# Feed-forward down products in pairs of slices, with seven block products for half of the columns

## The reference, cut to what matters

```
h = h + 0.5 * (silu(u @ wg) * (u @ wu)) @ wd        # u = rmsnorm(h), D = 1024, F = 2816
```

## Time and profile before

| | us |
|---|---|
| median of 3 runs | 1896.27 (1895.78 to 1896.41) |
| profiled execution, span | 1894.6 |
| its own time beside the span | not given; the median is 1.7 above the span |
| PE busy, DVE busy, ACT busy | 1874.1, 1229.6, 945.6 |

### The profile page before, as it was taken

The page is one execution under the profiler, slowest core; times in us unless marked ns, Lnnn a source line. Parts: engine busy times, 40 slices in busy tenths (PEclk is TensorE's granted clock), DMA queues, the critical chain, the costliest instruction groups (busy, mean ns, idle before and its releaser), DMA issues.

```text
span 1894.6 us, 34284 instructions
## 1 busy us (share of the span) xinstructions
PE 1874.1 (99%) x13508; PEld 1745.4 (92%) x13508; DVE 1229.6 (65%) x1654; ACT 945.6 (50%) x1301; POOL 66.1 (3%) x94
## 2 busy tenths in 40 slices
PE   9999999999999999999999999999999999999998
PEld 8999999999998889999999998999999998889998
DVE  5666765675556647666765699765676665877665
ACT  5444544454446636444544457644454446455443
POOL 0000100000000000000100000100010002010000
PEclk9999999999999999999999999999999999999999
DMA  7555455545453245555555443565545453344552
GB/s 282 199 191 184 164 199 199 189 165 207 185 198 134 68 149 215 191 183 194 200 199 198 146 145 111 201 233 199 189 167 203 185 199 126 130 152 178 192 199 100
DMA packets 61505, 338.60 MB, mean 179 GB/s; under 512 B 6976, under 2 KB 7360, under 8 KB 33024
## 3 DMA queue, kind: packets, MB, share of 16 engines
q1 hardware_dynamic: 59472, 330.00, 47.3%
q0 software_dynamic: 1968, 7.70, 1.2%
HBM read 336.62 MB, written 1.05 MB: 178 GB/s over the span
## 4 chain that ended last, share of the span: by engine, by line
PE 93%; DVE 3%; ACT 2%; issue 1%; POOL 1%; DMA 1%; SPq 0%; DVEq 0%; ACTq 0%; POOLq 0%
PE X L1698 55%; PE Y L1698 36%; DMA rawA<-in_wa 1%; ACT hiA L590 1%; PE X L1739 1%; ACT arena L804 0%; DVE arena L1481 0%; DVE xs L1193 0%; DVE h L1200 0%; DVE xl L1145 0%; PE Y L2213 0%; DVE loA L1105 0%; DVE arena L1418 0%; POOL ms_eps L489 0%; PE X L1722 0%
## 5 line engine op out<-in xcount | busy, mean ns | idle before, releaser
L1698 PE MATMUL X<-xh,hiA 128*128 128x256 f32 x2464 | 679.0, 277 | 1.7 <-DVE loA L1091 0.8
L1698 PE MATMUL X<-xl,hiA 128*128 128x256 f32 x2464 | 677.4, 277 | 0.0
L1698 PE MATMUL X<-xh,loA 128*128 128x256 f32 x2464 | 668.9, 277 | 0.0
L1105 DVE TENSOR_TENSOR loA<-rawA,hiA 128x2048 fp32r<-128x2048 f32 x213 | 487.9, 2290 | 265.2 <-ACT hiA L590 265.0
L1698 PEld LDWEIGHTS X<-xh,hiA 128*128 128x128 f32 x2464 | 462.7, 188 | 3.2 <-DVE loA L1091 1.7
L1698 PEld LDWEIGHTS X<-xl,hiA 128*128 128x128 f32 x2464 | 463.3, 188 | 0.0
L1698 PEld LDWEIGHTS X<-xh,loA 128*128 128x128 f32 x2464 | 457.1, 188 | 0.0
L590 ACT ACTIVATE hiA<-rawA 128x2048 fp32r<-128x2048 f32 (+1 forms) x239 | 424.0, 1776 | 46.1 <-PE Y L1698 29.8
L708 ACT ACTIVATE act_s<-act_s 128x256 f32<-128x256 f32 x154 | 64.4, 418 | 427.2 <-DVE act_s L1257 427.2
L1698 PE MATMUL Y<-hiB,act_hh 128*128 128x512 f32 x704 | 275.5, 391 | 0.9 <-DVE act_hl L1270 0.9
L1698 PE MATMUL Y<-hiB,act_hl 128*128 128x512 f32 (+1 forms) x880 | 275.9, 346 | 0.0
(11 more groups left out here) (263 smaller groups left out, 2217.8 us busy)
## 6 DMA issues: line engine op xcount, KB each, us to landing
rawA<-in_wa SPq DMA_DIRECT2D x221, 1024.0 KB, 5.4
rawB<-in_wb SPq DMA_DIRECT2D x181, 512.0 KB, 3.5
row_gain<-in_rows POOLq DMA_DIRECT2D x8, 512.0 KB, 6.1
arena<-in_gla POOLq DMA_DIRECT2D x1, 1280.0 KB, 5.8
h<-in_x SPq DMA_DIRECT2D x2, 512.0 KB, 4.0
arena<-in_taps POOLq DMA_DIRECT2D x1, 576.0 KB, 5.7
arena<-in_pool POOLq DMA_DIRECT2D x1, 544.0 KB, 6.6
rawA<-in_wa SPq DMA_DIRECT2D x2, 256.0 KB, 5.9
```

What stands on the lines that cost most here:

```text
L1105: nc.vector.tensor_tensor(loA[p][:, :], rawA[p][:, :], hiA[p][:, :].bitcast(f32), ALU.subtract).then_inc(a_lo, 1)
L1698: return say(nc.tensor.matmul(*args, **kw))
```

## The change

Slice 0 and the slices 19, 20, 21 are done as before. The 18 slices between go in PAIRS = 9 pairs (1,2), (3,4) ... (17,18), on PE: gate_up of the next odd slice, gate_up of the next even one, then the down products of a pair.

The right 512 output columns of a pair are done as before, undivided in the last matmul. The left 512 form a product of 2 x 2 blocks (2 token halves, 2 slices; 2 slices, 2 column blocks of 256), done by seven block products instead of eight, in Winograd's form of Strassen's scheme. DVE makes four sums of weights (T1 to T4, the first two in one operation) and four of activations (S1 to S4); ACT and DVE split them in high and low parts too, which lie in xh and xl or oh2 and ol2, whichever the stage doesn't use. Three of the seven products go straight to their places in Y; four are collected in X banks 2 and 3 over all nine pairs (the one in X[:, 2, 0:256] goes into all four places of the result). Once in each feed-forward `fold` forms the sums of the collected blocks that the four places need, splits them, and PE adds them into Y by four matmuls of 512 with the identity.

Gate and up of a slice now share one bank of X, and DVE scales both in one operation after up. act_hh, act_hl, hiB and loB are made for both slices of a pair in one operation. The SP queue loads in the order A, B, B, A. In ffn0 the weighing of the pool weights stands in the last period, before the scaling of slice 20. The copy of ident_r moves on POOL from the stage before the latent attention to the start of the kernel; the wait before the latent keys and before the attention's scores counts one less.

```diff
+        def gate_bank(p):
+            return X[:, p, 0:TOKENS]
+        def up_bank(p):
+            return X[:, p, TOKENS:2 * TOKENS]
+        sums_w = xs[:, 1, :].rearrange("p (a b) -> p a b", b=TOKENS)
+        sums_act = xs[:, 0, 0:512].rearrange("p (a b) -> p a b", b=P)
+        fold_raw = xs[:, 1, :]
+        fold_tmp = xs[:, 0, 512:512 + TOKENS]
...
+        def spare(s):
+            pair = (xh, xl) if s["reuse"] else (oh2, ol2)
+            return [v.rearrange("p a b -> p (a b)") for v in pair]
+        def pair_w(s, i):
+            return [v[:, TOKENS * i:TOKENS * (i + 1)] for v in spare(s)]
+        def pair_act(s, i):
+            return [v[:, 1024 + P * i:1024 + P * (i + 1)] for v in spare(s)]
...
+                    def later_loads(i):
+                        load_A(a + 4 + 2 * i, a % 2)
+                        load_B(b + 1 + 2 * i, (b + 1) % 2)
+                        load_B(b + 2 + 2 * i, b % 2)
+                        load_A(a + 5 + 2 * i, (a + 1) % 2)
+                    with sp.Fori(1, PAIRS) as i:
+                        later_loads(i)
+                    taken[0] = a + NF
+                    later_loads(PAIRS)
+                    load_B(b + NF - 1, (b + 1) % 2)
...
+                    nc.gpsimd.tensor_copy(ident_r[:, :], ident[:, :]).then_inc(ident_r_set, 1)
...
+                def pair_hi(i):
+                    act.wait_ge(prod_done, e + 1 + 2 * i)
+                    act.wait_ge(b_free, b + 1 + 2 * i)
+                    nc.scalar.activation(act_hh[:, :, :], act_h[:, :, :], ACT.Copy).then_inc(prod_hi, 2)
+                    act.wait_ge(pair_sums, SUMS * (pairs + i))
+                    nc.scalar.activation(act_sum_hi, sums_act.rearrange("p a b -> p (a b)"), ACT.Copy
+                                         ).then_inc(sum_act_hi, 1)
+                    for f in (1, 2):
+                        act.wait_ge(b_loaded[(b + f) % 2], loads(b + f - 2 + 2 * i, (b + f) % 2))
+                    nc.scalar.activation(hiB_both[:, :, :], rawB_both[:, :, :], ACT.Copy).then_inc(b_hi, 2)
+                    nc.scalar.activation(w_hi, sums_w.rearrange("p a b -> p (a b)"), ACT.Copy).then_inc(sum_w_hi, 1)
+                def period(i):
+                    pair_hi(i)
+                    silu(2 * i + 1, 1)
+                    split_A(a + 3 + 2 * i, (a + 1) % 2)
+                    silu(2 * i + 2, 0)
+                    split_A(a + 4 + 2 * i, a % 2)
...
+                period(PAIRS)
+                product_hi(NF - 3, 1, NF - 1)
+                nc.scalar.activation(fold_raw[:, TOKENS:2 * TOKENS], X[:, 2, 0:TOKENS], ACT.Copy).then_inc(fold_copied, 1)
+                split_B(b + NF - 3, (b + 1) % 2)
+                product_hi(NF - 2, 0, NF - 1)
+                for half in range(2):
+                    act.wait_ge(fold_sums, 4 * s["ffn"] + 2 + 2 * half)
+                    nc.scalar.activation(w_hi[:, HALF[half]], fold_raw[:, HALF[half]], ACT.Copy).then_inc(fold_hi, 1)
+                split_B(b + NF - 2, b % 2)
+                silu(NF - 1, 1)
+                product_hi(NF - 1, 1, NF)
+                split_B(b + NF - 1, (b + 1) % 2)
+                split_A(a + NF + 1, (a + 1) % 2)
...
+                def scaled(f, p, opened=False):
                     if s["late"]:
...
                         dve.wait_ge(up_psum, e + 1 + f)
...
+                        both = X[:, p, :].rearrange("p (a b) -> p a b", b=TOKENS)
...
+                def weight_sums(i):
+                    if not (isinstance(i, int) and i == 1):
+                        dve.wait_ge(sum_w_lo, pairs - 1 + i)
+                    for f in (1, 2):
+                        dve.wait_ge(b_loaded[(b + f) % 2], loads(b + f - 2 + 2 * i, (b + f) % 2))
+                    flat = rawB_both.rearrange("p a b -> p (a b)")
+                    taken = flat[:, TOKENS:TOKENS + 1536].rearrange("p (a b) -> p a b", b=768)[:, :, 0:TOKENS]
+                    upper = rawB[0][:, 0:TOKENS].rearrange("p (a b) -> p a b", a=1).broadcast_to([P, 2, TOKENS])
+                    nc.vector.tensor_tensor(sums_w[:, 0:2, :], upper, taken, ALU.subtract).then_inc(pair_sums, 1)
+                def act_sums(i):
+                    done = SUMS * (pairs - 1 + i)
+                    def after(n):
+                        dve.wait_ge(pair_sums, done + n)
+                    if not (isinstance(i, int) and i == 1):
+                        dve.wait_ge(sum_act_lo, pairs - 1 + i)
+                    a11, a21 = (act_h[:, one, P * t:P * t + P] for t in range(TT))
+                    a12, a22 = (act_h[:, two, P * t:P * t + P] for t in range(TT))
+                    dve.wait_ge(prod_done, e + 1 + 2 * i)
+                    nc.vector.tensor_tensor(sums_act[:, S1, :], a21, a22, ALU.add).then_inc(pair_sums, 1)
+                    nc.vector.tensor_tensor(sums_act[:, S3, :], a21, a11, ALU.subtract).then_inc(pair_sums, 1)
+                    after(1)
+                    nc.vector.tensor_tensor(sums_w[:, T2, :], rawB[1][:, 0:TOKENS], sums_w[:, T1, :], ALU.subtract
+                                            ).then_inc(pair_sums, 1)
+                    after(2)
+                    nc.vector.tensor_tensor(sums_act[:, S2, :], sums_act[:, S1, :], a11, ALU.subtract).then_inc(pair_sums, 1)
+                    after(4)
+                    nc.vector.tensor_tensor(sums_w[:, T4, :], rawB[1][:, TOKENS:2 * TOKENS], sums_w[:, T2, :], ALU.subtract
+                                            ).then_inc(pair_sums, 1)
+                    after(5)
+                    nc.vector.tensor_tensor(sums_act[:, S4, :], a12, sums_act[:, S2, :], ALU.subtract).then_inc(pair_sums, 1)
...
+                def period(i, last=False):
+                    split_A(a + 2 + 2 * i, a % 2)
+                    dve.wait_ge(prod_hi, e + 1 + 2 * i)
+                    nc.vector.tensor_tensor(act_hl[:, :, :], act_h[:, :, :], act_hh[:, :, :].bitcast(f32),
+                                            ALU.subtract).then_inc(prod_lo, 2)
+                    dve.wait_ge(sum_act_hi, pairs + i)
+                    nc.vector.tensor_tensor(act_sum_lo, sums_act.rearrange("p a b -> p (a b)"), act_sum_hi.bitcast(f32),
+                                            ALU.subtract).then_inc(sum_act_lo, 1)
+                    dve.wait_ge(b_hi, b + 1 + 2 * i)
+                    nc.vector.tensor_tensor(loB_both[:, :, :], rawB_both[:, :, :], hiB_both[:, :, :].bitcast(f32),
+                                            ALU.subtract).then_inc(b_lo, 2)
+                    dve.wait_ge(prod_lo, e + 1 + 2 * i)
+                    scaled(2 * i + 1, 1)
+                    dve.wait_ge(sum_w_hi, pairs + i)
+                    nc.vector.tensor_tensor(w_lo, sums_w.rearrange("p a b -> p (a b)"), w_hi.bitcast(f32),
+                                            ALU.subtract).then_inc(sum_w_lo, 1)
+                    product(2 * i + 1, 1)
+                    split_A(a + 3 + 2 * i, (a + 1) % 2)
+                    if last and a == 0 and plan[1]["kind"] == "pool":
+                        weigh_pooling(plan[1]["a"])
+                    scaled(2 * i + 2, 0)
                     if not last:
+                        weight_sums(i + 1)
+                    product(2 * i + 2, 0)
+                    if not last:
+                        act_sums(i + 1)
...
+                def fold():
+                    done = 4 * s["ffn"]
+                    p5, p6, p7 = X[:, 2, TOKENS:2 * TOKENS], X[:, 3, 0:TOKENS], X[:, 3, TOKENS:2 * TOKENS]
+                    place = [fold_raw[:, TOKENS * q:TOKENS * (q + 1)] for q in range(4)]
+                    dve.wait_ge(b_free, b + NF - 1)
+                    dve.wait_ge(sum_w_lo, pairs + PAIRS)
+                    dve.wait_ge(fold_copied, s["ffn"] + 1)
+                    nc.vector.tensor_tensor(fold_tmp, place[1], p6, ALU.add).then_inc(fold_sums, 1)
+                    dve.wait_ge(fold_sums, done + 1)
+                    nc.vector.tensor_tensor(place[0], fold_tmp, p5, ALU.add).then_inc(fold_sums, 1)
+                    nc.vector.tensor_tensor(place[3], fold_tmp, p7, ALU.add).then_inc(fold_sums, 1)
+                    dve.wait_ge(fold_sums, done + 3)
+                    nc.vector.tensor_tensor(place[2], place[3], p5, ALU.add).then_inc(fold_sums, 1)
+                def fold_low():
+                    for half in range(2):
+                        dve.wait_ge(fold_hi, 2 * s["ffn"] + half + 1)
+                        nc.vector.tensor_tensor(w_lo[:, HALF[half]], fold_raw[:, HALF[half]],
+                                                w_hi[:, HALF[half]].bitcast(f32), ALU.subtract).then_inc(fold_lo, 1)
...
+                product_lo(0, 0)
+                if s["reuse"]:
+                    latent_lo()
+                split_A(a + 2, a % 2)
+                scaled(1, 1)
+                product(1, 1)
+                split_A(a + 3, (a + 1) % 2)
+                scaled(2, 0)
+                weight_sums(1)
+                product(2, 0)
+                act_sums(1)
```

(108 more changed lines are left out.)

125 lines of the change are left out of this document (66 added, 59 removed).

## The result

The changed kernel takes **1919.05 us**, median of 4 runs (1918.37 to 1919.62), against 1896.03 (1895.24 to 1896.41) for the kernel before beside it: ratio 1.0119, 95% interval 1.0105 to 1.0133. It is slower by 23.0 us. The forecast was 1886.3, faster by 10.0, with 1897.0 as the top of its range: wrong in sign, and by 32.8 us in size. The profiled execution's span went from 1894.6 to 1916.6 us.

What follows compares the result with a forecast made beforehand. PE's matmul starts were taken as the bound: -25.1 us (pairs), +7.3 (fold), +2.1 (beginning), +5.3 (tail), +0.9 (ffn0), -0.5 (old tail wait) gave -10.0, hence 1886.3 us; 8 in 10 range 1879 to 1897.

Steps and rivals of the forecast that it cites:

- The step that failed: PE's steady period: starts cost 0.445 ns a column at either width, so two slices' gate and up take 10.92 us.
- The narrow products: Left half of a pair's down products: 21 matmuls of 256 columns at 0.1138 us each, 2.39 us.
- rival 4: In the pairs, 256-wide down matmuls start slower than gate/up's: 9.5 us if all 21 do, 1895.8, no change; 8%.
- Rival 5: On PE, each matmul has a price apart from its columns: at 30 ns each 19 us, 1906; 1%.
- The gain of seven for eight: Pairs' down products on PE: 5.13 us instead of 5.48, 0.35 less, over 72 pairs -25.1 us.
- The cover in the middle: Steady pairs: DVE's 14.3 us and ACT's 8.8 hide within PE's 16.05 us period, least margin 3.5 us.
- Rival 1: Steady pairs: B loads become the loop if two land over 7.1 us after issue; at 7.5 us, 1909; 9%.
- The two ends: Feed-forward's beginning and tail: PE waits 0.3 us (+2.1 in all) and 0.75 us (+5.3), plus 0.9 in ffn0.
- the tail's walk: After the last pair, a chain through DVE and ACT makes PE wait 0.75 us at slice 21, 7 times: +5.3.
- Rivals 2 and 3: Feed-forward ends: either they cost nothing (1878, 9%), or 2.5 us more a feed-forward (1904; half of that 1895; 12%).

Runs made afterwards that it cites:

- experiment 1: The kernel before, with the last down matmul of each slice left undivided as one of 512 columns: 1924.18 us, ratio 1.0145.
- experiment 4: The changed kernel with each pair's narrow products first, then its twelve wide matmuls, the last one divided into two of 256: 1893.45 us, ratio 0.9984.
- 3: The changed kernel with each pair's narrow products first, then its twelve wide matmuls, all undivided: 1919.16 us, ratio 1.0118.
- experiment 2: The changed kernel with the last wide matmul of a pair divided in its old place, ahead of the narrow products: 1920.12 us, ratio 1.0123.
- 7: The kernel before, with both the last and the last but one down matmul of a slice divided: 1898.30 us, one run.
- 6: The kernel before, with the division moved to the last but one of a slice's twelve down matmuls: 1898.25 us, one run.
- 5: The kernel before, with the division moved from the last to the first of a slice's twelve down matmuls: 1929.25 us, one run.

## Why the prediction was wrong, point by point

**The step that failed** is the one on which the period's sum stands: "The cost goes by columns, 0.445 ns each, at either width", and from it "10.92 of gate and up of the two next slices". It read the pitch of the earlier trace rows as a property of a 256-wide matmul. It is a property of that sequence: the same matmuls take 113.4 to 113.9 ns or 117.8, by what stands ahead of them, and in the changed kernel the 96 of two slices take 11.31 us and not 10.92. The change "removed" the division of the last wide matmul; I counted it as the same columns in one start less, at no cost and no gain, and gave it no bounds. Taken away alone in the kernel before, it costs 27.8 us (experiment 1); put back near gate in the changed one it gives 25.7 (experiment 4 against 3). Put back in its old place it gives nothing (experiment 2, 1920.12 us): the change had also put 21 narrow matmuls between it and gate, and either of the two would have been enough for the long rhythm. Bounds for it could have been had from the trace: the same shape at its other pitch, 0.19 us a slice.

**The narrow products** (forecast 2.39 us a pair) take 2.48. That is rival 4, which I had at 8% and 9.5 us: 120 ns were feared, 118 measured, (2.48 - 2.39) x 72 = 6.5 us. Its row, the start at 0.12 us after a change of width, was the right hint; that whole stretches of gate and up could run so stood in no rival. Gate and up alone lose 8 x 0.39 + 0.19 us a feed-forward, 26.5 us in all, more than the gain of 25.1 that the pairs were to bring, and that decides the sign. A row against the rule was in the trace of before all along, 5.65 us for 48 starts, outside the loop on which the sum was made.

**Rival 5**, a price of each matmul apart from its columns, isn't the cause: most of the loss lies in gate and up, which got no start more, and in experiment 1 one start less made the kernel slower. That a start is free is not shown, though. One start more went with 0.01 us more in experiment 2 against the changed kernel (2.77 against 2.76), 0.02 in the kernel before against 1 (2.74 against 2.72), and nothing in 7 against 6 (2.75 both). The largest step is 5 against 1, both long: 1929.25 against 1924.18 us, 5.1 us for 160 starts, some 32 ns each, with one run of 5. The prediction's count was wrong as well: a pair has 33 starts against 26, seven more and not nine, 504 in all, and the fold's 32 make the 536. An estimate from the gap figures of the Trainium skill (TensorE: Matmul & The Clock Gate, Back-to-back issue gap) had the pair's products cost 0.49 us more than before. They cost 5.24 against 5.48, and no run here bears those figures out.

**The gain of seven for eight** was right in sign: with the short rhythm in gate and up and long narrow matmuls the prediction's sum is 1886.3 + 6.5 = 1892.8, and experiment 4 measured 1893.45.

**The cover in the middle** held. The timeline of DVE (start, duration, engine, line, operation):

```profile
101.28 2.29 DVE L1423 TENSOR_TENSOR loB<-rawB,hiB 128x2048 fp32r<-128x2048 f32 x1 [1.03 <-ACT hiB L782]
...
104.40 1.21 DVE L1428 TENSOR_TENSOR ol<-xs,oh 128x1024 fp32r<-128x1024 f32 x1
...
106.77 2.29 DVE L1203 TENSOR_TENSOR loA<-rawA,hiA 128x2048 fp32r<-128x2048 f32 x1 [0.82 <-ACT hiA L651]
...
110.05 0.68 DVE L1386 TENSOR_TENSOR xs<-rawB 128x512 f32<-128x512 f32 x1
```

Here T = 97.94 (the gate in the timeline of PE above). loB at T+3.3, forecast 3.2; the low part of the weight sums ends at T+7.7, forecast 7.4; loA of the odd slice starts at T+8.8, forecast 8.6; weight sums at T+12.1. The period has no wait of PE for any of them. DVE was busy 13.50 us of it, not 14.3: the forecast added up whole durations, though operations that follow each other directly overlap by 0.08 us. **Rival 1** is out with it: the B loads were there when the weight sums wanted them.

**The two ends** came out as walked. What PE waited for, in the changed kernel:

```profile
PEld Y L1908 <- DVE loB L1215: 5.2, 8, 1.0
...
PEld X L1908 <- DVE loA L1203: 2.1, 7, 0.4
```

These rows count how long the weight loads stood idle, which begins before PE itself is late. What PE lost is read from its starts. Slice 21's first down matmul in ffn1, behind its forerunner, first in the changed kernel:

```profile
390.71 0.39 PE L1908 MATMUL Y<-hiB,act_hl 128*128 128x512 f32 x1
391.34 0.50 PE L1908 MATMUL Y<-hiB,act_hh 128*128 128x512 f32 x1 [0.24 <-DVE loB L1215]
```

and in experiment 4:

```profile
384.92 0.39 PE L1908 MATMUL Y<-hiB,act_hl 128*128 128x512 f32 x1
385.77 0.50 PE L1908 MATMUL Y<-hiB,act_hh 128*128 128x512 f32 x1 [0.47 <-DVE loB L1215]
```

A start is 0.23 us behind its forerunner when nothing waits. In the changed kernel it is 0.63 and the next one 0.34, so PE lost 0.51 us, in six feed-forwards alike; in ffn0 it lost 0.85, in ffn2 under 0.1. That is 3.9 us without ffn2, where 5.3 + 0.9 were forecast. The chain itself came out as walked: with T the first start of gate 21 (379.51 and 373.95) the matmul stands at T+11.83 and T+11.82, forecast 11.9. PE only reached it 0.19 us late, because gate and up of slice 21 ran long. With the short rhythm (experiment 4) PE lost 0.62 + 0.11 = 0.73 us, forecast 0.75. So the tail's walk was right, and the agreement of 5.2 with 5.3 is luck, since the two are different things. At the beginning, the 144 starts of slices 2 to 4 take mostly 16.70 us where inputs are scaled late and 16.34 in ffn2: 0.36 us a time, forecast 0.3. Rivals 2 and 3 are both out: the ends cost about what was said, and reordering the tail got 5 us back.

## What to carry to other kernels

A pitch read from a trace belongs to the sequence it was read in. Before a change takes away or moves even one matmul at a seam between groups, look in the whole trace for the same shape at another pitch, and carry both values through the sum; here 4 ns on 256-wide starts outweighed the eighth product that was saved. A split that looks redundant (one wide matmul issued as two halves) may be doing a job: take it away alone, and measure, before rewriting what stands around it.

## What the runs showed of the hardware that I had not expected

Gate and up, 256-wide matmuls with a weight load each, run at one of two pitches, 113.4 to 113.9 ns or 117.7 to 117.8, at full granted clock and with the same duration of 0.28 us. Each holds through the 96 starts of two slices (11.31 us in all 64 places of the changed kernel), and the short one through the 144 of three. Wide matmuls take 228 ns a start, and 2.51 us / 11 and 2.76 us / 12 in the changed kernels, 228 and 230. In the loops tried here the short pitch came where one of the last two wide passes ahead of gate and up was divided into halves, and the long one came in every other case: no division, a division at the first of twelve, a division with 21 narrow matmuls behind it, and a shared stationary without a division. It does not depend on the number of matmuls, nor on DVE or ACT, whose work was the same in experiments 3 and 4 and untouched in 1.

The narrow matmuls of a pair don't follow this rule. They average 118 ns behind undivided wide ones (the changed kernel), behind a divided one (2) and right behind gate and up in the short rhythm (4). In the changed kernel the third product alone has 113 ns, between neighbours at 120. It differs from them in its operands: it is the only one of the seven that pairs summed activations with weights as loaded. Whether the operands, their places or the order set its pitch, no run here separates. What inside TensorE or its weight loads keeps the rhythm of gate and up is open too: no run changed the loads alone. How the 18 long ones of the 21 could be brought to the short pitch is open as well, which would be worth some 72 x (2.48 - 2.39) = 6.5 us, an estimate from the pair's 21 starts at either pitch.
